# Input projections as pairs of output tiles, with seven block products in place of eight, in a two-layer streaming encoder kernel

## What is computed

```
h = RMSNorm(x)
proj = h @ w_in                  # columns: q 512, k 128, v 128, nine slices of 512, 4 x 1024 merge logits
o_a = window attention of q, k, v (QK-norm, rotary, sinks)
o_b = multi-scale trailing-mean pooling of p, mixed per group
o_c = u * (position mixing of LayerNorm(v_sgu))
o_d = swish(LayerNorm(31-tap causal depthwise conv of a * sigmoid(b)))
out = x + (sum over n of sigmoid(merge_n) * ((o_n * silu(z_n)) @ w_branch_n)) @ w_out
```

## Time and profile before

| what | value |
|---|---|
| device time, median of 3 runs | 2315.6 us (2315.27 to 2316.09) |
| profiled execution, first to last instruction | 2314.0 us, 1.6 us under the median of the runs |
| PE, PEld busy | 98%, 80% |
| DVE, POOL, ACT busy | 50%, 41%, 21% |
| mean granted clock of PE | 0.996 |
| HBM read, written | 131.6 MB, 12.6 MB |

### The profile page before, as it was taken

How to read it: one execution, slowest core, us unless ns; L and a number is a source line. 1 busy time by engine, 2 the same in 40 slices (tenths; PEclk the granted TensorE clock), 3 DMA queues, 4 the chain that set the end, 5 groups by cost and what they waited for, 6 DMA issues and landing times.

```text
span 2314.0 us, 30796 instructions
## 1 busy us (share of the span) xinstructions
PE 2274.9 (98%) x10370; PEld 1859.4 (80%) x10370; DVE 1154.9 (50%) x1068; ACT 491.1 (21%) x850; POOL 937.2 (41%) x852
## 2 busy tenths in 40 slices
...
PEclk9999999999999999999999999999999999999999
...
GB/s 217 50 50 41 42 46 42 41 44 47 50 51 46 46 50 41 118 50 73 136 94 50 50 40 43 42 42 41 46 47 49 51 46 50 50 37 123 45 97 117
DMA packets 72369, 141.18 MB, mean 61 GB/s; under 512 B 8096, under 2 KB 8992, under 8 KB 72224
## 3 DMA queue, kind: packets, MB, share of 16 engines
...
...
## 4 chain that ended last, share of the span: by engine, by line
PE 81%; DVE 12%; DVEq 3%; issue 2%; ACT 1%; ACTq 0%; DMA 0%; SPq 0%
PE acc L324 72%; DVE conv L956 7%; PE aux L428 2%; PE acc L428 2%; DVEq L958 2%; DVE oc L856 1%; PE aux L480 1%; PE aux L464 1%; PE aux L513 1%; PE aux L473 1%; PE aux L499 1%; PE aux L490 0%; PE aux L410 0%; DVE sumsq L859 0%; DVEq L956 0%
## 5 line engine op out<-in xcount | busy, mean ns | idle before, releaser
L300 POOL TENSOR_SCALAR whi<-raw 128x512 fp32r<-128x512 f32 x424 | 302.3, 713 | 1330.3 <-PE acc L324 973.9
L324 PE MATMUL acc<-hhi,whi 128*128 128x512 f32 x2496 | 809.2, 395 | 10.9 <-DVE xm L859 3.8
L324 PE MATMUL acc<-hlo,whi 128*128 128x512 f32 x2496 | 795.7, 390 | 0.0
L324 PE MATMUL acc<-hhi,wlo 128*128 128x512 f32 x2496 | 794.8, 389 | 0.0
L303 POOL TENSOR_TENSOR wlo<-raw,whi 128x512 fp32r<-128x512 f32 x424 | 635.1, 1498 | 35.4
L324 PEld LDWEIGHTS acc<-hhi,whi 128*128 128x128 f32 x2496 | 465.9, 188 | 117.8 <-issue 19.2
L324 PEld LDWEIGHTS acc<-hlo,whi 128*128 128x128 f32 x2496 | 469.1, 188 | 99.0 <-issue 1.2
L324 PEld LDWEIGHTS acc<-hhi,wlo 128*128 128x128 f32 x2496 | 468.6, 188 | 98.7
L956 DVE SCALAR_TENSOR_TENSOR conv<-conv,par x240 | 366.4, 1527 | 45.1 <-issue 45.1
L324 PE MATMUL acc<-bhi,whi 128*128 128x512 f32 x512 | 159.1, 392 | 0.0
L324 PE MATMUL acc<-blo,whi 128*128 128x512 f32 x512 | 157.7, 389 | 0.0
...
## 6 DMA issues: line engine op xcount, KB each, us to landing
raw<-wstream SPq DMA_DIRECT2D x424, 256.0 KB, 2.6
...
```

The source lines that it names most:

```text
L300: nc.gpsimd.tensor_scalar(whi[:, i, :], raw[:, i % RAWS, :], 1.0, 0.0, ALU.mult, ALU.add).then_inc(hi_split, 1)
L324: mm = nc.tensor.matmul(acc[:, p, t * HALF:(t + 1) * HALF], w, m[:, kbase + k, t * HALF:(t + 1) * HALF], start=first and k == 0 and n == 0 ...
```

## The change

**Blocks.** h is cut into four blocks: channels 0 to 511 and 512 to 1023 (rows 1 and 2), tokens 0 to 511 and 512 to 1023 (columns). Two output tiles a and b make a pair. With four weight blocks and four blocks of h a pair needs eight products of 12 matmuls (4 blocks of 128, three matmuls each); Strassen's scheme in Winograd's form takes seven. For it DVE makes four combinations of the blocks of h once in a layer (`form`), POOL makes four combinations of weight blocks for every pair, and DVE adds the products up out of PSUM in five instructions of x512 per pair (`sum_x`, `sum_v`, `sum_22`, `sum_12`, `sum_21`); p1 with p2 is accumulated in the bank. All 32 pairs per layer do so: U 2, ZC 2, MC 4, GLU 4, ZA 2, MA 4, P 2, ZB 2, MB 4, ZD 2, MD 4. The four banks a, b, c, d of `acc` are single: a product waits until its bank was taken.

**Weights.** 232 units per layer, six `raw` buffers. The rounding to `whi` goes from POOL to ACT (`high`, an ACT copy of x512 that waits until the form four before was used); POOL keeps the subtraction (`low`) and gains the sums: four per pair, and in MA and MB four more per pair (`add_block`), which add the previous merge to this one. DVE no longer has the second instruction of `merge_tile`.

**Branch sums in memory.** The running sum of the branches goes by block of 128x512 from `prev` to DRAM and back (SP's queue), and is loaded as a whole in MD.

**q, k, v.** They are made with tokens on the partitions, h as the stationary operand: q in matmuls of 128x512 as before, k and v together in matmuls of 128x256 (384 of these in all). Normalising and rotating come first, then 32 transposes of q and 8 of k per layer; q goes through DRAM. The LayerNorm gains of the gating unit are folded into the position mixing, for which a ones-matmul per layer gives row sums.

**Order.** VS0, VS1, Q1, KV1, Q0, KV0, U, ZC, MC with attention, GLU, ZA, MA, P, ZB, MB, ZD, MD, O. The taps stand at 10 per pair in GLU 1 to 3, 6 per pair in ZA and ZB, 14 per pair in MA and 14 in MB 0. There are no engine loops; all is unrolled. The matmuls of each product, the branch products (12 matmuls per tile and half) and the output projection are otherwise the same.

The core of the diff:

```diff
+RAWS = 6
...
+PLAIN = (("VS0", 8), ("VS1", 8), ("Q1", 8), ("KV1", 4), ("Q0", 8), ("KV0", 4))
+STAGES = (("U", 2), ("ZC", 2), ("MC", 4), ("GLU", 4), ("ZA", 2), ("MA", 4), ("P", 2), ("ZB", 2), ("MB", 4),
+          ("ZD", 2), ("MD", 4))
...
+PROD = ("p1", "p6", "p5", "p2", "p7", "p3", "p4")
+BLOCKS = ("B11", "B12", "B22", "B21")
+BANK_OF = {"p1": "a", "p6": "b", "p5": "c", "p2": "a", "p7": "b", "p3": "c", "p4": "b",
+           "B11": "d", "B12": "a", "B22": "c", "B21": "d"}
+TAKEN_BEFORE = {"p1": 0, "p6": 0, "p5": 0, "p2": 1, "p7": 1, "p3": 1, "p4": 2,
+    "B11": 0, "B12": 2, "B22": 2, "B21": 1}
...
+        OPERAND = {"p1": S_B11, "p6": S_F6, "p5": S_F5, "p2": S_B21, "p7": S_F7, "p3": S_B22, "p4": S_F4}
...
-    nc.gpsimd.tensor_scalar(whi[:, i, :], raw[:, i % RAWS, :], 1.0, 0.0, ALU.mult,
-                            ALU.add).then_inc(hi_split, 1)
-    pool.wait_ge(hi_split, n + 1)
-    nc.gpsimd.tensor_tensor(wlo[:, i, :], raw[:, i % RAWS, :],
-                            whi[:, i, :].bitcast(F32), ALU.subtract).then_inc(unit_split, 1)
...
+def low(L, src, *key):
+    f = L * FORMS + FORM[key]
+    pool.wait_ge(hi_made, f + 1)
+    nc.gpsimd.tensor_tensor(wlo[:, f % SLOTS, :], src, whi[:, f % SLOTS, :].bitcast(F32),
+                            ALU.subtract).then_inc(lo_made, 1)
...
+            w21, w22 = loaded(L, st, i, "w21"), loaded(L, st, i, "w22")
+            first, second = wsum[:, 0, :], wsum[:, 1, :]
+            pool.wait_ge(lo_made, split(L, st, i, "p1") - 1)
+            add(first, w21, w22, sums_made)
+            w11 = loaded(L, st, i, "w11")
+            pool.wait_ge(sums_made, sum_n(L, st, i, 1))
+            add(second, first, w11, sums_made)
+            low(L, w11, st, i, "p1")
+            low(L, second, st, i, "p6")
+            if before:
+                add_block(L, *before, "B11")
+            low(L, first, st, i, "p5")
+            add(w21, w21, w11, sums_made)
+            if before:
+                add_block(L, *before, "B12")
+                add_block(L, *before, "B22")
+            w12 = loaded(L, st, i, "w12")
+            low(L, w12, st, i, "p2")
+            pool.wait_ge(lo_made, split(L, st, i, "p2"))
+            add(first, second, w12, sums_made)
+            if before:
+                add_block(L, *before, "B21")
+            low(L, w21, st, i, "p7")
+            low(L, first, st, i, "p3")
+            low(L, w22, st, i, "p4")
+            if st in MERGES:
+                low(L, loaded(L, st, i, "bA"), st, i, "bA")
+                low(L, loaded(L, st, i, "bB"), st, i, "bB")
+            before = (st, i) if st in ("MA", "MB") else None
...
+def pair(L, st, i, between=None):
+    between = between or {}
+    for q in PROD + (BLOCKS if st in MERGES else ()):
+        if q in between:
+            between[q]()
+        bank = BANK_OF[q]
+        name = {"B11": "bA", "B12": "bA", "B22": "bB", "B21": "bB"}.get(q, q)
+        slot = (L * FORMS + FORM[st, i, name]) % SLOTS
+        if (st, i) == ("U", 0) and q in ("p6", "p5", "p7", "p4"):
+            pe.wait_ge(form_ready, L * 8 + {"p5": 2, "p7": 4, "p6": 6, "p4": 8}[q])
+        pe.wait_ge(lo_made, split(L, st, i, name))
+        pe.wait_ge(taken[bank], bank_n(L, bank, (st, i), TAKEN_BEFORE[q]))
+        if q in PROD:
+            s = OPERAND[q]
+            mm = three(BANK_AP[bank], fhi[s], flo[s], slot, 0, q not in ("p2", "p4"), True,
+                       resumed=q in ("p2", "p4"))
+        else:
+            t = PLACE[q][1]
+            if q == "B11":
+                pe.wait_ge(gated, gates_before(L, "Z" + st[1]) + 8)
+            mm = three(BANK_AP[bank], bhi, blo, slot, 0, True, True, slice(t * HALF, (t + 1) * HALF))
+        mm.then_inc(step_done, 1)
...
+            for e in range(per):
+                kk = k * per + e
+                s = H_SLOT[kk // UK, t]
+                at = slice(tile * P, (tile + 1) * P)
+                w_at = slice(e * width, (e + 1) * width)
+                for m, (h, w) in enumerate(((fhi, whi), (flo, whi), (fhi, wlo))):
+                    mm = nc.tensor.matmul(dst, h[s][:, kk % UK, at], w[:, f % SLOTS, w_at],
+                                          start=kk == 0 and m == 0, stop=kk == KT - 1 and m == 2)
...
+def begin_pair(L, st, i, after=None):
+    act.wait_ge(step_done, stepped(L, st, i, "p1"))
+    copy(xs[:, i % 2, :], BANK_AP["a"]).then_inc(taken["a"], 1)
+    next_high(L, st, i, "p1")
+    if after and "p1" in after:
+        after["p1"]()
+    next_high(L, st, i, "p6")
+    if after and "p6" in after:
+        after["p6"]()
+    next_high(L, st, i, "p5")
+    if after and "p5" in after:
+        after["p5"]()
+    act.wait_ge(step_done, stepped(L, st, i, "p2"))
...
+def squash(L, st, i, q, func):
+    bank, k, buf = {"C22": ("b", 2, y1[:]), "C12": ("c", 2, v1[:]), "C21": ("b", 3, xs[:, i % 2, :])}[q]
+    act.wait_ge(taken[bank], bank_n(L, bank, (st, i), k))
+    nc.scalar.activation(buf, buf, func).then_inc(squashed, 1)
+def squash_first(L, st, i, func):
+    nc.scalar.activation(s1[:], BANK_AP["a"], func).then_inc(taken["a"], 1)
...
+def gate_pair(L, st, i, src, after=None):
+    begin_pair(L, st, i, after)
+    squash_first(L, st, i, ACT.Silu)
+    next_high(L, st, i, "p2")
+    squash(L, st, i, "C22", ACT.Silu)
+    next_high(L, st, i, "p7")
+    branch_rounded(L, st, i, "C11", src)
+    squash(L, st, i, "C12", ACT.Silu)
+    next_high(L, st, i, "p3")
+    branch_rounded(L, st, i, "C22", src)
+    squash(L, st, i, "C21", ACT.Silu)
+    next_high(L, st, i, "p4")
+    branch_rounded(L, st, i, "C12", src)
+    branch_rounded(L, st, i, "C21", src)
...
+        merge_pair(L, "MC", i, {"p1": lambda L=L, i=i: exps(L, 2 * i),
+                                "p4": lambda L=L, i=i: exps(L, 2 * i + 1)})
...
+def form(L, n):
+    at = slice(n % 2 * 2, n % 2 * 2 + 2)
+    b11, b12, b22, b21 = (q[:, at, :] for q in (x11, x12, x22, x21))
+    if n < 2:
+        op = sub(b11, b11, b12)
+    elif n < 4:
+        op = sub(b12, b22, b12)
+    elif n < 6:
+        op = scaled(b22, b22, -1.0, b11, ALU.subtract)
+    else:
+        op = scaled(b21, b22, -1.0, b21, ALU.subtract)
+    op.then_inc(form_made, 1)
...
+def sum_x(L, st, i):
+    x_ = xs[:, i % 2, :]
+    dve.wait_ge(taken["a"], bank_n(L, "a", (st, i), 1))
+    dve.wait_ge(step_done, stepped(L, st, i, "p6"))
+    add(x_, x_, BANK_AP["b"]).then_inc(taken["b"], 1)
+def sum_v(L, st, i):
+    dve.wait_ge(step_done, stepped(L, st, i, "p5"))
+    dve.drain()
+    add(v1[:], xs[:, i % 2, :], BANK_AP["c"]).then_inc(taken["c"], 1)
+def sum_22(L, st, i, dst):
+    dve.wait_ge(step_done, stepped(L, st, i, "p7"))
+    dve.drain()
+    scaled(dst, v1[:], -1.0, BANK_AP["b"], ALU.subtract).then_inc(taken["b"], 1)
+def sum_12(L, st, i, dst):
+    dve.wait_ge(step_done, stepped(L, st, i, "p3"))
+    dve.drain()
+    add(dst, v1[:], BANK_AP["c"]).then_inc(taken["c"], 1)
+def sum_21(L, st, i, dst):
+    dve.wait_ge(step_done, stepped(L, st, i, "p4"))
+    dve.drain()
+    scaled(dst, xs[:, i % 2, :], -1.0, BANK_AP["b"], ALU.subtract).then_inc(taken["b"], 1)
 convf = conv[:].rearrange("p s t -> p (s t)")
+def taps(L, n0, n1):
+    for n in range(n0, min(n1, WT * TAPS)):
+        j, k = n // TAPS, n % TAPS
+        o = convf[:, j * SW + PADC:(j + 1) * SW]
+        at = (j + 1) * SW + PADC - (TAPS - 1) + k
+        h = convf[:, at:at + SEQ]
+        w = allp[:, L, C_CW + j * TAPS + k:C_CW + j * TAPS + k + 1]
+        dve.drain()
+        if k == 0:
+            nc.vector.tensor_scalar(o, h, w, allp[:, L, C_CB + j:C_CB + j + 1], ALU.mult, ALU.add)
+        else:
+            scaled(o, h, w, o, ALU.add)
...
+def gate_pair(L, st, i, src, tap0=0, tap_n=0, after_v=None):
+    n = [tap0 + tap_n * e // 6 for e in range(7)]
+    taps(L, n[0], n[1])
+    sum_x(L, st, i)
+    taps(L, n[1], n[2])
+    if (st, i) == ("ZD", 0):
+        dve.wait_ge(merge_added, merges_before(L, "MB") + 14)
+    sum_v(L, st, i)
+    if after_v:
+        after_v()
+    taps(L, n[2], n[3])
+    gate(L, st, i, "C11", src)
+    if (st, i) == ("ZD", 0):
+        dve.wait_ge(merge_added, merges_before(L, "MB") + 16)
+    sum_22(L, st, i, y1[:])
+    gate_rest(L, st, i, "C11", src)
+    taps(L, n[3], n[4])
+    gate(L, st, i, "C22", src)
+    sum_12(L, st, i, v1[:])
+    gate_rest(L, st, i, "C22", src)
+    taps(L, n[4], n[5])
+    gate(L, st, i, "C12", src)
+    sum_21(L, st, i, xs[:, i % 2, :])
+    gate_rest(L, st, i, "C12", src)
+    taps(L, n[5], n[6])
+    gate(L, st, i, "C21", src)
+    gate_rest(L, st, i, "C21", src)
+def merge_block(L, st, i, q):
+    n = BLOCKS.index(q)
+    bank = BANK_OF[q]
...
+def merge_sums(L, st, i, between):
+    sum_x(L, st, i)
+    between[0]()
+    if st in ("MA", "MB") and i:
+        dve.wait_ge(merge_added, merges_before(L, st) + 4 * i - 2)
+    sum_v(L, st, i)
+    between[1]()
+    if st in ("MA", "MB") and i:
+        dve.wait_ge(merge_added, merges_before(L, st) + 4 * i)
+    sum_22(L, st, i, y1[:])
+    between[2]()
+    sum_12(L, st, i, v1[:])
```

(23 more changed lines are left out.)

2091 lines of the change are left out of this document (1232 added, 859 removed).

## The result

The changed kernel takes 2398.5 us (median of 4 runs, 2396.1 to 2399.5) against 2315.7 for the kernel before on the same chip: 1.0354 times as long, 95% interval 1.034 to 1.0369. The prediction was 2287, with a range of 2200 to 2362. It failed in direction and in range.

What follows compares the result with a forecast made beforehand. The prediction took PE, busy 98% of the span, to bound the kernel. PE's 2133.8 us, 124 for turns of DVE and POOL, 8 and 20 for new waits and 1.6 around the span made 2287 us, range 2200 to 2362.

Steps and rivals of the forecast that it cites:

- PE does less: Matmuls and transposes in all layers: 180.2 us saved on PE, from the profiled span 2314.0 to 2133.8 us.
- rival 4: q, k, v: matmuls of x256 cost the full 0.227 us; +41 us, 2328 in all; chance 0.06.
- Turns of the taps: GLU, ZA, MA, P 1, ZB, MB 0: DVE's two-SBUF instructions and POOL take turns; +124 us, between 107 and 148.
- Rival 1: Pairs with taps: no turns, the lag dissolves; 2163 us, with some remnant up to 2215; chance 0.14.
- The floor of this term, if the engines took no turns, is nothing: GLU and MA: without turns DVE's free time is 19.0 us in GLU and 26.0 in MA, so no lag.
- rival 2: Gate pairs: DVE waits for ACT, 7.2 us per pair; 70 us in all, 2357; chance 0.24 with other piled-up waits.
- likeliest sum: Whole kernel: 2133.8 + 124 + 8 + 20, and 1.6 around the span, 2287 us; own range 2242 to 2311.
- The pooling tiles: P 1 and ZB: tiles on DVE delay PE, 3 us per layer in P 1, 4 to 5 in ZB.
- new waits: MC 8 us in all (0 to 20); U 0, ZD 0, P 0 and O 20 us, between 0 and 40.
- Rival 3: Lagging pairs: after each wait the granted clock falls, 2.2 us lost each, 53 us in all, 2340; chance 0.10.
- ZC and ZD pairs over 22 us with DVE idle for ACT: ZC and ZD: sign named ahead that the forecast is wrong and rival 2 holds.

Runs made afterwards that it cites:

- e1: Changed kernel with the taps' running sum in PSUM in place of SBUF (13 taps per layer keep both inputs in SBUF): 2295.0 us.
- e5: Kernel of e1 with each remainder of a gated block (gate_rest) one sum later on DVE: 2213.3 us.
- e8: Changed kernel with only each remainder of a gated quarter one sum later on DVE, taps keeping both inputs in SBUF: 2318.2 us.
- e2: Changed kernel with 30 of the 31 taps of each tile left out: 2252.9 us, one run.
- e10: Kernel of e5 with the window sums and 16 edge columns left out of each pooling tile, one x1024 instruction remaining: 2181.5 us, one run.
- e3: Changed kernel without POOL's four weight sums per pair, the products taking single weight blocks: 2309.9 us, one run.
- e4: Changed kernel with 20 to 32 unused matmuls ahead of p6 in GLU 2, GLU 3, ZA 0, ZA 1 and MA 0: 2398.0 us, one run.

## Why the prediction was wrong

Its sum was 2133.8 + 124 + 28 + 1.6. Against it the runs put, term by term:

- **PE does less: right.** 0.227 and 0.120 us as taken, instructions as counted; rival 4 is out. The Trainium skill's 131 ns for 512 columns ("TensorE: Matmul & The Clock Gate", Back-to-back issue gap) would have made the saving 74 us smaller; the rows above show 227 ns again.
- **Turns of the taps: right in mechanism and nearly in size.** 124 us held two parts: the pooling tiles (3 in P 1, 4 to 5 in ZB, so 15 in two layers), and 109 for taps. The taps' turns measured 103.5 (e1) or 104.9 (e5 against e8). GLU 2 and 3, predicted 5.6 to 6.7 over PE's time, came to 7.6, of which 1.5 stay in e1 (as they do in e5); MA 1 to 3, predicted 4.2 to 6.2 over, came to 4.2 to 7.2. Rival 1 (no turns) is out. What the prediction had at nothing is DVE's time without turns ("The floor of this term, if the engines took no turns, is nothing"): in e5, GLU 2, GLU 3, ZA 0, ZA 1 and MA 0 still lie 1.5, 1.5, 1.5, 1.9 and 3.9 us over PE's time in layer 0, some 20 us in both layers. It goes with the taps (GLU 2, GLU 3 and ZA 0 take 19.0 in e2) and is counted in the last term below.
- **DVE waits for ACT in gate pairs: the step that failed.** The prediction worked this out as rival 2 at 7.2 us per gate pair, gave it 0.24, and left it out of the likeliest sum: "POOL works meanwhile, and DVE's lag gives ACT time". The trace shows 102.3 / 16 = 6.4 us of wait per pair, so the size was good. But the argument against it does not hold: what ACT's queue has ahead of the rounding is a squash that needs DVE's own next sum, so however late DVE is, the round trip starts only when DVE gets there. POOL's turns did not fall into these waits either: the order is worth the same 80 and 82 us with and without the taps' turns, and the waits themselves are 102.3 us with them and 99.6 without (e1). The likeliest sum should have had it: 80 of the 111 us by which it missed.
- **The pooling tiles: mis-sized by 17.** 15 us were taken, e10 shows 32. P 1 was priced at 3 us per layer, as the tile's wait behind three products; it took 10.7 over PE's 22.5 in the changed kernel and 9.6 in e5, and these go with the windows in e10; ZB 0's was 5.7 where 4 to 5 were taken. The prediction saw one tile in P 1, the one in front of `sum_22`, which takes 12.0 us of DVE in the changed kernel; the tile of P 0 stands in front of `sum_x` of P 1 and takes 12.3 more, and PE waits for both at the mixings, not at bank b. Behind each wait PE mixes at 1.2 GHz (granted clock 0.50 from 729.0 to 732.3 and from 742.6 to 745.9 us), 3.64 us in place of the 1.88 of e10. The two mixings of P 1, first in the changed kernel, then the second one in e10:

```profile
728.97 3.64 PE L751 MATMUL aux<-pt,pmix 128*128 128x512 f32 x4 [2.46 <-DVE pt L1569]
742.39 3.64 PE L751 MATMUL aux<-pt,pmix 128*128 128x512 f32 x4 [4.32 <-DVE pt L1569]
```

```profile
671.59 1.88 PE L751 MATMUL aux<-pt,pmix 128*128 128x512 f32 x4
```

Together, 6.8 us of waits and 3.5 of slower mixing are 10.3 of the 10.7. At the second mixing the clock does cost time, since PE sets the pace there: `sum_21` on DVE waits 5.0 us for it.

- **The rest: 46 where 28 were taken for new waits.** The 46 are what is left: 2398.5 less 2135.4, 103.5, 81.7 and 31.8, so they hold more than new waits. About 20 are DVE's own time, named above. MC was well priced: 1.1 us in the pairs MC 1 to 3 against 1 taken, but 4.2 in MC 0 (2.5 with the order of e5), 14.9 in all (11.5) against 8. U 0 lies 6 us per layer over its 19.0 and 1.8 of transposes, against 2; without weight sums (e3) it is 0.4, so 5.7 per layer come from the rotations' turns with POOL, and the prediction had priced turns for taps and gated products alone. The kernel before has 35.7 us of waits of its own inside the 2135.4, so these parts need not add up to 46; what remains wasn't isolated.

So -5.5 + 81.7 + 16.8 + 18 makes the 111 us. Of the rivals, 2 was the case and too cheap in its total (2357), by 41 us: 12 in its own term, which was put at 35 us per layer where 41 came, and 29 in the terms around it. Rival 3 (the clock) looked right on the page, with 206 us at 1.2 GHz, but e4 gave 72 of them back for nothing. For the pairs that e4 doesn't touch it stays open as an after-effect of the waits, and the second mixing of P 1 shows one. What the prediction held against it, that the waits should be pieces of 1 to 3 us, was wrong in part: the longest was 8.3, and p6 of GLU 2 waited 5.3 and then ran at 1.2 GHz for some 4 us. But these were waits for DVE, which went on meanwhile.

The signs named ahead were good ones: "ZC and ZD pairs over 22 us with DVE idle for ACT (rival 2)" is what ZC 1 (23.7) and ZD 1 (25.9) show; ZC has no tap in it, so this needed no run.

The change's own saving is real. With two edits that leave its computation as it is, PSUM for a running sum and three remainders a step later, the same kernel takes 2213.3 us, and with a pooling tile moved and the taps spread anew 2202.3 to 2203.7: 4.8 to 4.9% under the kernel before.
